# Loading x in pieces of 256, 256 and 512 features, and starting the first projection on features 0 to 255

## What is computed

```python
def rms_norm(x, gain):
    xf = x.astype(jnp.float32)
    y = xf * lax.rsqrt(jnp.mean(xf * xf, axis=-1, keepdims=True) + EPS)
    return (y * gain.astype(jnp.float32)).astype(x.dtype)
...
        hn = rms_norm(x, norm1_g[l])
        proj = hn @ w_in[l]
        qa, ka, va = [proj[..., i * WIDTH_A:(i + 1) * WIDTH_A].reshape(b, s, N_HEADS_A, HEAD_DIM)
                      for i in range(3)]
```

## Time and profile before

| what | us |
|---|---|
| median of 3 runs | 1567.67 |
| lowest and highest | 1566.78, 1567.79 |
| the profiled execution's own time | 1567.44 |
| its span in the profile | 1565.7 |
| TensorE (PE) busy in the span | 1558.1 |
| ScalarE, VectorE, POOL busy | 691.2, 645.1, 751.0 |

### The profile page before, as it was taken

One profiled execution on the slowest core, in us unless ns is written; L12 is line 12 of the kernel. 1 busy time (PEld: TensorE's weight loads), 2 busy tenths in 40 slices (PEclk: granted clock), 3 DMA queues, 4 the chain that ended last, 5 costly groups with the idle time before them and its releaser, 6 DMA issues.

```text
span 1565.7 us, 23287 instructions
## 1 busy us (share of the span) xinstructions
PE 1558.1 (100%) x8010; PEld 1255.4 (80%) x8010; DVE 645.1 (41%) x1081; ACT 691.2 (44%) x1194; POOL 751.0 (48%) x577
## 2 busy tenths in 40 slices
PE   9999999999999999999999999999999999999999
PEld 7877777888888888888878887778888888888887
DVE  5345465244355544220488544542432222210234
ACT  5565554334444443332543654754353333322342
POOL 6632465543544454444587333334554444444441
PEclk9999999999999999999999999999999999999999
DMA  6422222222433333333333224222333333333331
GB/s 186 144 77 57 68 75 61 88 86 83 121 86 89 107 101 100 95 101 88 81 95 96 76 62 135 68 69 77 105 96 100 98 97 94 114 95 98 97 94 62
DMA packets 103352, 145.60 MB, mean 93 GB/s; under 512 B 11109, under 2 KB 57166, under 8 KB 103134
## 3 DMA queue, kind: packets, MB, share of 16 engines
q1 hardware_dynamic: 103102, 142.30, 31.2%
q10 hardware_dynamic: 160, 2.11, 0.4%
HBM read 142.24 MB, written 2.13 MB: 92 GB/s over the span
## 4 chain that ended last, share of the span: by engine, by line
PE 98%; DVE 1%; DMA 0%; issue 0%; SPq 0%; ACT 0%; DVEq 0%
PE bank L1693 89%; PE bank L1601 2%; PE bank L1630 2%; PE bank L1618 2%; PE bank L1848 1%; DMA xtok<-in_x 0%; PE bank L1679 0%; PE bank L1871 0%; PE bank L1888 0%; PE bank L1824 0%; PE bank L1909 0%; PE bank L1882 0%; PE bank L1825 0%; PE bank L1896 0%; PE bank L1715 0%
## 5 line engine op out<-in xcount | busy, mean ns | idle before, releaser
L688 POOL TENSOR_TENSOR w_lo<-w_raw,w_hi 128x512 fp32r<-128x512 f32 x516 | 696.1, 1358 | 784.8 <-ACT w_hi L897 784.1
L897 ACT ACTIVATE w_hi<-w_raw 128x512 fp32r<-128x512 f32 x516 | 319.1, 628 | 660.2 <-PE bank L1693 590.0
L1693 PE MATMUL bank<-h_hi,w_lo 128*128 128x512 f32 x1244 | 489.1, 393 | 0.3 <-DVE fq L1156 0.3
L1693 PE MATMUL bank<-h_hi,w_hi 128*128 128x512 f32 x1244 | 484.4, 389 | 0.0
L1693 PE MATMUL bank<-h_lo,w_hi 128*128 128x512 f32 x1244 | 484.2, 389 | 0.0
L1693 PEld LDWEIGHTS bank<-h_hi,w_lo 128*128 128x128 f32 x1244 | 233.5, 188 | 51.9 <-issue 3.3
L1693 PEld LDWEIGHTS bank<-h_hi,w_hi 128*128 128x128 f32 x1244 | 233.5, 188 | 48.8
L1693 PEld LDWEIGHTS bank<-h_lo,w_hi 128*128 128x128 f32 x1244 | 233.7, 188 | 47.2
L1281 DVE TENSOR_TENSOR bank<-bank,rstd 128x512 f32<-128x512 f32 x88 | 60.1, 700 | 261.5 <-PE bank L1693 261.5
L1693 PE MATMUL bank<-g_hi,w_lo 128*128 128x512 f32 x352 | 137.0, 389 | 0.0
L1693 PE MATMUL bank<-g_hi,w_hi 128*128 128x512 f32 x352 | 136.9, 389 | 0.0
(11 more groups left out here) (297 smaller groups left out, 1764.0 us busy)
## 6 DMA issues: line engine op xcount, KB each, us to landing
w_raw<-in_w_in SPq DMA_DIRECT2D x168, 256.0 KB
w_raw<-in_w_ffn_up SPq DMA_DIRECT2D x88, 256.0 KB
w_raw<-in_w_ffn_down SPq DMA_DIRECT2D x88, 256.0 KB
w_raw<-in_w_ffn_gate SPq DMA_DIRECT2D x88, 128.0 KB
w_raw<-in_w_ffn_up SPq DMA_DIRECT2D x88, 128.0 KB
w_raw<-in_w_out SPq DMA_DIRECT2D x32, 256.0 KB
w_raw<-in_w_branch_a SPq DMA_DIRECT2D x16, 256.0 KB
w_raw<-in_w_branch_b SPq DMA_DIRECT2D x16, 256.0 KB
```

What stands on the lines that cost most here:

```text
L688: e.tensor_tensor(w_lo[:, pos % SPLIT_SLOTS, :], w_raw[:, pos % RAW_SLOTS, :], w_hi[:, pos % SPLIT_SLOTS, :].bitcast(F32), ALU.subtract).t ...
L897: e.activation(w_hi[:, pos % SPLIT_SLOTS, :], w_raw[:, r, :], ACT.Copy).then_inc(hi_full, 1)
L1693: mm = e.matmul(ps[banks + n][:, :], l, r, start=k == 0 and i == 0, stop=k == p.kc - 1 and i == 2)
```

## The change

x is loaded in twelve transfers instead of four: first features 0 to 255 of all four token blocks, then weight slot 0, then features 256 to 511 of all blocks, then weight slot 1, then features 512 to 1023, then the other slots. Only the transposes of chunks 0 and 1 stand ahead of slot 0. Those of chunks 2 and 3 come behind slot 0, those of 4 to 7 behind slot 2 (the new step "turn"). All transposes now go through banks 4 to 7, so slot 0 no longer waits for the copies to free its banks. ScalarE squares the blocks behind the rounding of slot 3, and VectorE makes all of `sum_hi` and `sum_lo` ahead of `h_lo` of chunk 4, and copies chunks 5 to 7 one by one behind that. The sums' matmuls and `rstd` move from behind slot 5 to behind slot 6. Some semaphores that nothing used are gone.

```diff
@@ make_schedule @@
     run(["qA", "kA", "vA", "qB", "kB", "vB", "gateA", "branchA", "gateB"],
-        [(5, ("sumsq", 0)), (5, ("rstd", 0)), (9, ("rtok", 0)), (8, ("vec", 1)), (13, ("masks",))]
+        [(0, ("turn", 2, 4)), (2, ("turn", 4, 8)), (6, ("sumsq", 0)), (6, ("rstd", 0)), (9, ("rtok", 0)), (8, ("vec", 1)), (13, ("masks",))]
...
@@ bank_uses @@
         if x[0] == "start":
-            take(("vec", 0), 7)
-            for j in range(4, 8):
-                take(("x", j), j)
+            for j in range(2):
+                take(("x", j), 4 + j)
+        elif x[0] == "turn":
+            for j in range(x[1], x[2]):
+                take(("x", j), 4 + j % 4)
...
@@ SyncE @@
+            def load_x(tb, piece):
+
+                c = slice(*((0, 256), (256, 512), (512, 1024))[piece])
+                e.dma_start(xtok[:, tb, c], a["x"][0, tb * P:(tb + 1) * P, c]).then_inc(x_full[tb] if piece == 0 else x_later[piece - 1], 16)
+
             for tb in range(TB):
-                e.dma_start(xtok[:, tb, :], a["x"][0, tb * P:(tb + 1) * P, :]).then_inc(x_full[tb], 16)
+                load_x(tb, 0)
...
                             load(p.name, g, k, p.slot0 + g * p.kc + k)
+                            if p.name == "qA" and k < 2:
+                                for tb in range(TB):
+                                    load_x(tb, k + 1)
...
@@ ScalarE @@
             def first_square(tb):
 
-                e.wait_ge(x_full[tb], 16)
-                e.activation(x_squares[:, tb, :], xtok[:, tb, :], ACT.Square, accum_out=xstat[:, tb:tb + 1]).then_inc(x_sums, 1)
+                e.wait_ge(x_later[0], 16 * TB)
+                e.wait_ge(x_later[1], 16 * TB)
+                if tb >= 2:
+                    e.wait_ge(x_sums, tb - 1)
+                e.activation(x_squares[:, tb % 2, :], xtok[:, tb, :], ACT.Square, accum_out=xstat[:, tb:tb + 1]).then_inc(x_sums, 1)
...
                     uses("natural_log_exp")
-                    for tb in range(TB - 1):
-                        first_square(tb)
                     hi(0, 0)
                     e.wait_ge(gains_ready, 1)
                     first_unscaled(0)
+                    hi(1, 1)
+                    first_unscaled(1)
+                    hi(2, 2)
                     first_copied(3)
-                    for j in range(1, DC):
+                    first_unscaled(2)
+                    first_unscaled(3)
+                    hi(3, 3)
+                    first_square(0)
+                    first_square(1)
+                    hi(4, 4)
+                    first_square(2)
+                    first_square(3)
+                    for j in range(4, DC):
                         first_unscaled(j)
-                        hi(j, j)
-                        if j == 4:
-                            first_square(TB - 1)
+                        if j > 4:
+                            hi(j, j)
...
@@ VectorE @@
-                    for j in range(3):
-                        first_copied(j)
-                    for j in range(4):
-                        first_lo(j)
-                        first_copied(4 + j)
-                    first_lo(4)
+                    first_copied(0)
+                    first_copied(1)
+                    first_lo(0)
+                    first_lo(1)
+                    first_copied(2)
+                    first_lo(2)
+                    first_lo(3)
+                    first_copied(4)
+                    e.wait_ge(x_sums, TB)
                     for tb in range(TB):
-                        e.wait_ge(x_sums, tb + 1)
-
                         c = slice(tb * P, (tb + 1) * P)
...
                     ins.then_inc(sum_lo_ready, 1)
+                    first_lo(4)
                     for j in range(5, DC):
+                        first_copied(j)
                         first_lo(j)
...
@@ TensorE @@
                     for tb in range(TB):
                         e.wait_ge(x_full[tb], 16)
-                        for j in range(DC - 1):
+                        for j in range(2):
                             turned(j, tb)
...
+                elif what == "turn":
+                    e.wait_ge(x_later[x[1] // 4], 16 * TB)
+                    for j in range(x[1], x[2]):
+                        bank_wait(e, ("x", j))
+                        for tb in range(TB):
+                            turned(j, tb)
...
                         if prev is None:
-                            if n == 3:
-                                e.wait_ge(x_last, 1)
-                            else:
-                                e.wait_ge(x_rest, n + 1)
+                            e.wait_ge(gains_ready, 1)
```

More of the change, by code:

```diff
@@ L405, in two_block_kernel @@
         xtok = u("xtok", 0, [P, TB, D])
-        x_squares = u("x_squares", 48, [P, TB, D])
+        x_squares = u("x_squares", 48, [P, 2, D])
         vrows = u("vrows", 16, [P, 3, P])
@@ L475, in two_block_kernel @@
         x_full = [sem(f"x_full{tb}") for tb in range(TB)]
+        x_later = [sem(f"x_later{i}") for i in range(2)]
         gain_full = sem("gain_full")
@@ L494, in two_block_kernel @@
         A = {kind: {n: sem(f"{n}{kind}") for n in (
-            "sc_done", "s_ready", "e_ready", "r_ready", "p_ready", "tr_done", "pv_done", "yhi", "ylo")}
+            "sc_done", "s_ready", "p_ready", "tr_done", "pv_done", "yhi", "ylo")}
             for kind in "BAF"}
+        for kind in "AF":
+            A[kind] |= {n: sem(f"{n}{kind}") for n in ("e_ready", "r_ready")}
         A["B"] |= {n: sem(f"{n}B") for n in ("keep_ready", "beta_ready", "after_ready")}
@@ L499, in two_block_kernel @@
         up_sem = {n: {k: sem(f"{n}_{k}") for k in (
-            "scaled", "first", "conv1", "conv2", "silu", "prod", "hi", "lo")} for n in ("up1", "up2")}
+            "scaled", "first", "conv1", "silu", "prod", "hi", "lo")} for n in ("up1", "up2")}
         hgs = {n: sem(f"hg_{n}") for n in (
@@ L1434, in first_copied @@
                 e.wait_ge(xt_done, j + 1)
-                link(e.tensor_copy(xT[:, j, :], ps[j][:, :]))
+                bank = 4 + j % 4
+                link(e.tensor_copy(xT[:, j, :], ps[bank][:, :]))
                 e.nop().then_inc(x_rest, 1)
-                if j >= 4:
-                    e.nop().then_inc(bank_free[j], 1)
+                e.nop().then_inc(bank_free[bank], 1)
             def first_lo(j):
@@ L1462, in _ @@
                     e.wait_ge(vec_done, 1)
[L1463 to L1464 removed]
+                    link(e.tensor_copy(vec[:, 0:8], ps[0][:, 0:8]))
                     e.nop().then_inc(gains_ready, 1)
                     e.wait_ge(const_ready, 1)
[L1467 to L1472 removed]
+                    first_copied(0)
[7 more added lines that the diff above has]
+                    e.wait_ge(x_sums, TB)
                     for tb in range(TB):
[L1474 removed]
                         c = slice(tb * P, (tb + 1) * P)
@@ L1645, in operand, with turned @@
                 return x_hi[:, k, :], x_lo[:, k, :]
+            def turned(j, tb):
+                mm = e.transpose(ps[4 + j % 4][:, tb * P:(tb + 1) * P], xtok[:, tb, j * P:(j + 1) * P], ident[:, :])
+                if tb == TB - 1:
+                    mm.then_inc(xt_done, 1)
             def mean_square(norm):
@@ L1745, in _ @@
                     e.wait_ge(const_ready, 1)
-                    def turned(j, tb):
-                        mm = e.transpose(ps[j][:, tb * P:(tb + 1) * P], xtok[:, tb, j * P:(j + 1) * P], ident[:, :])
-                        if tb == TB - 1:
-                            mm.then_inc(xt_done, 1)
                     for tb in range(TB):
                         e.wait_ge(x_full[tb], 16)
-                        for j in range(DC - 1):
+                        for j in range(2):
                             turned(j, tb)
@@ L1757, in _ @@
                             e.wait_ge(gain_full, 16)
-                            e.transpose(ps[7][:, 0:8], vrows[0:8, 0, :], ident[0:8, 0:8]).then_inc(vec_done, 1)
-                        if tb == 1:
-                            bank_wait(e, ("x", 7))
-                            turned(7, 0)
-                        if tb:
-                            turned(7, tb)
-                    e.wait_ge(const_dve, 2)
+                            e.transpose(ps[0][:, 0:8], vrows[0:8, 0, :], ident[0:8, 0:8]).then_inc(vec_done, 1)
+                    e.wait_ge(const_dve, 2)
+                elif what == "turn":
[4 more added lines that the diff above has]
+                            turned(j, tb)
                 elif what == "vec":
```

9 lines of the change are left out of this document (5 added, 4 removed).

## The result

The changed kernel takes 1576.38 us in the median of 5 runs (1575.47 to 1576.72), the kernel before 1567.67. The ratio is 1.0054, with a 95% interval of 1.004 to 1.0067: slower by 8.7 us. The forecast, 1572.5, had the direction and the place right and the size wrong; 1576.0 was the upper end of its range.

A forecast was written before the change was run, and what follows sets the result against it. TensorE's own work and new waits ahead of it were taken as the bound. 0.5 us gained by slot 7's end and 5.3 lost waiting make slot 8 4.8 later: 1572.2, plus 0.23 for the median, 1572.5; range 1570 to 1576.

The forecast's parts named there:

- ScalarE becomes late: At the start: ScalarE copies chunk 3 at about 12.35 us and has the last sum of squares at 19.7.
- VectorE's sums stand ahead of chunk 4: Ahead of `h_lo` of chunk 4: VectorE's sums make TensorE wait 0.8 us at slot 4, then 0.7 at the next.
- POOL's slots 5 to 7 set when slot 14 may be loaded: POOL's remainders start at 24.95, 27.35, 29.75; slot 14 is loaded after 34.8 and rounded from 37.5, `rstd` behind it.
- The wait at slot 8: TensorE, idle from 34.9, waits 5.3 us for `rstd` and qA's first tile; slot 8 begins at 40.2.
- the landing of slot 2: At the start: weight slot 2 lands by 11.4 us, is rounded by 11.9, and does not delay chunk 3's copy.
- The bound of 0.8 us: At the start: moving 1 MB of x's short pieces at the lower rate costs 0.8 us, putting the copy at 12.6.
- the clock's term: After the long wait at slot 8: nothing added for a lowered TensorE clock, priced between nothing and 2.4 us.
- a rival with 0.27: At slot 8: same wait and the clock falls in it, 7.2 us at most, 1574.5 taken; chance 0.27.
- the plain case: At slot 8: the wait alone, no clock fall, makes it 4.8 us later; 1571 to 1574, chance 0.42.
- The weights are not that late: At slot 8: weights come sooner, `rstd` costs only 2 to 3 us, 1568 to 1570.5; chance 0.12.
- A clock that has not risen when slot 0 begins: At slot 0: it takes 5.4 us instead of 2.7, all behind up to 2.7 later, 1575.2; chance 0.15.
- Only the start counts: At slot 8: no wait for qA's first tile, slot 8 at 33.3 against 35.4, 1565.6; chance 0.04.

The follow-up runs named there:

- run 1: Changed kernel with the sums' matmuls and `rstd` behind slot 5 again, so behind slot 13's rounding; 1574.31 us, ratio 1.0044.
- run 2: Changed kernel with the sums' matmuls behind slot 5 and `rstd` right behind slot 7's rounding, ahead of all later roundings; 1568.85 us, ratio 1.0006.
- run 8: Changed kernel with VectorE making each block's sums as its square comes, copies of chunks 4 to 7 one ahead of the remainders; 1572.85 us.
- run 5: Changed kernel with weight slot 2 loaded ahead of the third pieces of x (features 512 to 1023); 1574.97 us, ratio 1.0046.
- Run 7: Changed kernel with x in two pieces (features 0 to 255, 256 to 1023) and slot 1 loaded ahead of the second; 1575.46 us, ratio 1.0052.
- run 4: Changed kernel with 22 unused matmuls of 512 columns on TensorE behind slot 7, filling the long wait; 1574.37 us, ratio 1.0041.
- run 6: Kernel before the change, with only the sums' matmuls and `rstd` moved from behind slot 5 to behind slot 6; 1568.52 us, ratio 1.0007.
- run 9: Changed kernel with slot 2 loaded earlier, `rstd` behind slot 7's rounding, and sums made as each square comes; 1566.20 us, ratio 0.999.
- run 10: The kernel of run 9 with five more warm-up matmuls on TensorE between the transposes of chunks 0 and 1 and slot 0; 1565.87 us, ratio 0.9986.
- run 3: Changed kernel with VectorE's small sum operations behind its last remainder and copies of chunks 5 to 7 one ahead; 1575.85 us, ratio 1.0051.

## Why the prediction was wrong in size and right in kind

**Right, by its steps.** Slot 0 at 8.64 (8.5 forecast). ScalarE becomes late and VectorE's sums stand ahead of chunk 4: TensorE started slot 4 0.8 us late (0.8) and slot 5 0.6 (0.7). POOL's slots 5 to 7 set when slot 14 may be loaded, and `rstd` stands behind slot 14's rounding: shown by runs 1, 2 and 8. The wait at slot 8 was 4.95 us between matmuls (5.3 from the last slot's end forecast). Its two ends were both late: slot 7 ended near 36.8 and not at 34.9, so that nothing was gained by then and 1.4 us lost, and slot 8 began at 41.91 and not at 40.2.

**Wrong: the landing of slot 2.** The step said that the same bytes stand ahead of slot 3 as before, so that slot 2 is there by 11.4 us and the rounding does not hold up the copy of chunk 3 at 12.35. It landed at 13.60, and the copy started at 14.16. The rate was not the same. The changed kernel up to 13.6 us, the kernel before up to 11.4, then two windows of the kernel before beside those of the changed one above:

```profile
0.00:13.60 13.60, 10.84 (x50) 9.18 (x51) 5.29 (x12) 3.89 (x5) 4.25 (x12) 1.00 0.77 244
0.00:11.40 11.40, 9.02 (x49) 7.89 (x49) 2.38 (x9) 5.76 (x9) 2.02 (x11) 1.00 0.77 272
6.00:7.00 1.00, 0.86 (x5) 0.43 (x4) 0.17 (x1) 0.21 (x1) 0.00 (x0) 1.00 1.03 307
9.00:10.00 1.00, 0.85 (x9) 0.62 (x7) 0.00 (x0) 0.60 (x2) 0.00 (x0) 1.00 1.05 406
```

At the same share, 0.77, 244 GB/s were moved and not 272. By 13.6 us 3.3 MB had been moved, 0.2 more than x and slots 0 to 3 together, so slot 4, issued at 12.05, and the small loads had taken part of the rate before slot 2 was complete. In the two slices 307 and 406 GB/s were moved before, 175 and 176 now. Run 5 takes slot 2 out of the way and wins 0.9 to 1.0 us at slot 8. The bound of 0.8 us was drawn from weight transfers late in the kernel, whose 294 GB/s had been scaled up from 97 at a share of 0.33; the pieces of x did worse. SyncE's issuing, which the prediction counted only against the small loads, put slot 2's issue at 7.77, but it did not starve the transfers on the whole: by then 2.6 MB were issued and 1.4 MB moved (174 GB/s over 7.77 us). Run 7 gives 0.65 us to shorter rows and fewer transfers together; how the rest divides among short rows, the number of transfers and how they follow each other stays open. Of the 1.8 us that the copy was late, POOL's slots 5, 6 and 7 were still 1.7, 1.45 and 1.3 late (26.61, 28.80, 31.01 against 24.95, 27.35, 29.75), since a chunk took 2.2 us and not 2.4; slot 8 was 1.7, with 0.3 more for slot 14's load (2.92 us to landing, 2.63 taken). The late landing also made the wait of 1.11 us ahead of slot 2, which the prediction does not have and run 5 takes away.

**Wrong: the clock's term.** The step was "I take nothing for the sum, since no row shows it drop"; the fall of the clock in the long wait stood as a rival with 0.27 and a price of up to 2.4 us. It fell in the changed kernel and in every variant that had such a wait (3.55 to 5.75 us), and run 4 took it away by filling the wait. It cost 2.6 us (slot 8 took 5.4 us instead of 2.8), of which run 4 gave 2 back. The Trainium skill's rule, page "TensorE: Matmul & The Clock Gate", section "Why this matters for your kernels", was on the side of this rival, and the trace agrees: 0.50 over slot 8. A missing row was read as evidence against it, while the kernel before had no idle time of that length that could have shown one.

Both terms together, 1.7 and 2.6, make the plain case's 4.8 into 9.1, the 9.1 measured at the end of slot 8. What is given back later, 0.5 us by the end of the span, was between 630 and 880 us, and run 6 has it as well (1.3 us late at slot 8's end, 0.6 at the end of its span), so it is no part of this change. The range allowed for one surprise at a time and hardly for both.

**The other rivals.** "The weights are not that late": they were later than forecast, slot 14 rounded at 39.10 and not 37.5. A clock that has not risen when slot 0 begins: not in the changed kernel's profile, whose slot 0 ran at 0.25 us a matmul. In runs 5, 7 and 9 it stood at 0.50 there, not because it had not risen but because it was low again behind the 1.7 to 2.0 us ahead of slot 0 (the last paragraph below). "Only the start counts": run 10 comes nearest. With `rstd` early, the weights sooner and the first idle time filled, slot 0 begins 4.0 us sooner than before (7.85 against 11.82) and the kernel takes 2 us less, since 24 transposes (2.6 us) no longer lie in the wait for x.

## What to carry to other kernels

When a load or a step is moved, follow what its engine's list then puts ahead of the next thing that the critical engine needs: here a rounding that waits for a weight transfer stood ahead of two activations of 1.2 us, and its lateness became theirs. Price a long idle time of TensorE twice, for its length and for the half clock behind it, even when the trace of before shows no fall because it has no such idle time. A gain at the start of a kernel bound by TensorE is worth only what no later wait takes back.

## What the runs showed of the hardware

The small operations of VectorE on SBUF took 0.28 to 0.35 us beside an idle POOL and 1.25 to 1.41 us each, eight in a row, beside POOL's unbroken work. That was seen at a few places before; that it multiplies a chain of eight by four was not expected.

TensorE's clock was at its lower level after the long wait in all six profiled executions that had one, from 3.55 to 5.75 us, and not after the 1.13 us of run 6; behind the 1.57 to 1.97 us ahead of slot 0 it was low in three executions (runs 5, 7 and 9) out of the nine with that gap. In those three the clock had risen before the last transposes (six weight loads in 0.64 us, against 1.1 where it had not); in two more with such early transposes, runs 2 and 3, it stayed up. So behind the same gap slot 0 took 4.4 to 4.5 us in some executions and 3.0 in others. In the whole time no cost of it can be seen: of the eleven executions of run 9 six had a mean clock of 0.999 and five of 1.000, with medians of 1566.3 and 1566.2 us, and all eleven of run 10 had 1.000.
